# Sample rows' projections on four 32-column tiles, and attention products that alternate the two key/value heads

## The chip, the cores and the metric

The kernel runs on one core of one Trainium2 chip. The metric is the time of one execution in device microseconds (us). Engines: PE (TensorE, matrix products), DVE (VectorE), ACT (ScalarE), POOL (GpSimd, here the issuer of the row gathers) and SP (SyncE, the issuer of the weight loads).

## The reference

One decoder layer for 512 prompt rows and 8 sample rows (one new token for each of eight sequences with a cache), all in float32, width 1024. Cut to what matters:

```python
sh1,sc1,g1,sh2,sc2,g2 = split6(silu(c) @ w_ada + b_ada)      # adaLN, one vector per sequence
h  = rms_norm(x) * (1+sc1) + sh1
q, k, v, p, ga, gb = split(h @ w_in)                         # 512, 128, 128, 512, 1024, 1024 columns
A  = sliding-window attention, 8 query heads on 2 key/value heads, head width 64, window 128
B  = multi-scale causal pooling of p
x  = x + g1 * ((sigmoid(ga)*(A@w_branch_attn) + sigmoid(gb)*(B@w_branch_pool)) @ w_out)
h2 = rms_norm(x) * (1+sc2) + sh2
x  = x + g2 * peer(h2)     # 8 heads x 16 experts a row, each a gathered row of two 16384 x 1024 tables
```

## The kernel before

**Stages.** The prompt is four blocks of 128 rows (`NB = 4`), the sample rows are a fifth block of eight (`rows(NB) = 8`). Activations for products lie transposed: `hT[:, k, cols(b)]` is the k-th of eight 128-row pieces of the width, for the columns of block b. The first part, to about 413 us, does adaLN, the projections, attention, pooling, the branches and the output projection of the first half of the prompt (256 rows), and the expert choice of the first heads. The second part gathers 1040 expert rows by indirect DMA from POOL, in an order fixed by index, while VectorE forms dot products and PE sums the expert rows (line 1531, on four 64 x 64 tiles) and does the second half's products.

**Order.** Every engine's program is written out by hand, and PE is in order. Results of PE go to eight PSUM banks in turn: `bank_plan()` lists all tiles in PE's order with the engine that empties them ("A" ScalarE, "V" VectorE), and `begin(key)` makes PE wait until the content eight places back is emptied. `wait_emptied` and `wait_filled` wait for one tile. Weights come in 2 MB chunks through a ring of three slots (`weight_chunks`, SP's loop, lines 462 to 483): SP, in order, loads a chunk as soon as the chunk three before in its slot has had its last product.

**Projections** (PE lines 1284 to 1292). For each of q, kv and p, five blocks; a block is eight products over k with `hT` as the stationary operand and 512 (kv: 256) weight columns streaming. The sample block streams the same columns for a stationary operand of eight columns. ScalarE copies each block out (line 591, the helper `empty`). Then the gate products (line 1296, by the helper `pass_product`, whose matmuls are on line 1227), two 128-row gates by two between the later steps. A float32 matmul is two instructions in the trace.

**q and k normalisation.** When all kv blocks are out, VectorE squares and sums (lines 902 to 904), ScalarE takes a root after the first four gates (line 632), VectorE multiplies (906 to 911) and sets `qk_normed`, which PE awaits on line 1299 before it transposes q and k, and POOL before its window stores.

**Attention of a block b.** PE makes scores (line 1318: operands of 64 rows, since a head is 64 wide; key/value head 0 lies on partitions 0 to 63, head 1 on 64 to 127). VectorE adds the bias into `sS[b % 2]` (922), finds maxima (928 to 931), ScalarE exponentiates eight heads (643), VectorE normalises (939). PE then transposes the probabilities ("pt", 1340), ScalarE copies them to `pT`, and PE multiplies them with the values ("o", 1344), 64 output partitions a head, and only then turns to the other head, since both use one `pT`. On PE the order is scores(1), pooled(1), gates, values(0), scores(2), and so on.

**Samples.** Scores with the cached keys ("sc4", line 1390), pooled branch ("y", 1401), branch products with the weights `wa` and `wb`, then the value products of the samples ("os", lines 1422 and 1423, 4 columns each, the second for the oldest cached row), adaLN chunk 7 and the output projection.

**The adaLN products** (line 1245) are already packed: `scT` has 32-column pieces, product k goes to output partitions 32 (k % 4) and up, so that four products lie side by side in the array, and `ada` (line 1253) adds the four partial sums by a product with the 0/1 matrix at `K_SEL`.

## Time and profile before

| | |
|---|---|
| median of 3 runs | 1910.24 us (1908.02 to 1910.49) |
| the profiled execution | 1913.8 us |
| its span, first to last instruction | 1911.9 us |
| PE busy | 1327.0 us, 69% |
| DVE busy | 1108.7 us, 58% |
| POOL busy | 1108.0 us, 58% |
| ACT busy | 258.6 us, 14% |
| mean granted TensorE clock | 0.82 of 2.4 GHz |

Busy shares are means over both parts of the kernel, whose limits differ. A line number is that of the program above; line 591 is ScalarE's helper for all copies out of PSUM and line 1227 PE's helper for most products, so their instructions are told apart by their place in time and their shape. The chain of work that ended last is followed back from the last instruction; a piece of PE in it means that PE, not a wait, set the time there.

### The profile page before, as it was taken

The page shows a single profiled execution, that of the slowest core. Times are in us where ns is not written, and L with a number is a line of the kernel's source. Part 1 is how long each engine was busy: PE and PEld are TensorE (multiplying, and loading weights), DVE is VectorE, ACT ScalarE, POOL GpSimd, SP SyncE. Part 2 cuts the span into 40 slices and gives each one's busy share as a digit, 9 for nine tenths or more (in the row PEclk, how much of TensorE's full clock was granted, in tenths as well). Part 3 has the DMA queues.
Part 4 walks back from the last instruction along what each step waited for, and adds up shares of the span by engine and source line. Part 5 has one row for each costly group of instructions (what it writes and reads, how often), then busy time and mean ns, then how long its engine had stood idle before and what let it go on. Part 6 is the DMA issues. An engine that isn't in the chain of part 4 may idle for free.

```text
span 1911.9 us, 19507 instructions
## 1 busy us (share of the span) xinstructions
PE 1327.0 (69%) x7067; PEld 672.8 (35%) x7067; DVE 1108.7 (58%) x2613; ACT 258.6 (14%) x489; POOL 1108.0 (58%) x1066
## 2 busy tenths in 40 slices
PE   5999899896778857645877655556555547764567
PEld 3547667585344423213444211111111112211122
DVE  5013331267656667767557667767777666686540
ACT  2114430221111100111111101000000011100000
POOL 1201000036766677765677777777777777777773
PEclk8999897798799978788889876676667788777769
DMA  9334143869999999997999999999999999999996
GB/s 329 109 100 148 60 137 110 306 244 318 374 372 403 373 399 405 400 404 277 387 371 379 389 408 397 400 377 404 355 407 407 406 405 408 408 370 362 388 409 268
DMA packets 196265, 639.21 MB, mean 334 GB/s; under 512 B 21856, under 2 KB 23188, under 8 KB 196042
## 3 DMA queue, kind: packets, MB, share of 16 engines
q0 software_dynamic: 154992, 550.65, 74.6%
q1 hardware_dynamic: 41178, 87.31, 13.1%
q8 instruction: 57, 0.93, 0.2%
q14 instruction: 38, 0.31, 0.0%
HBM read 634.09 MB, written 3.59 MB: 334 GB/s over the span
## 4 chain that ended last, share of the span: by engine, by line
POOL 36%; PE 30%; DMA 15%; issue 12%; DVE 4%; ACT 2%; SPq 0%; DVEq 0%; POOLq 0%; ACTq 0%
POOL arena L543 36%; PE psum L1227 12%; DMA arena<-in_peer_v,arena 10%; PE psum L1531 7%; PE psum L1291 5%; DMA arena<-in_peer_u,arena 3%; PE psum L1245 1%; ACT arena L591 1%; DVE arena L1121 1%; DMA arena<-in_w_ada 1%; ACT arena L643 1%; PE psum L1318 1%; DMA arena<-in_w_in 1%; PE psum L1557 0%; DMA arena<-in_x_sample 0%
## 5 line engine op out<-in xcount | busy, mean ns | idle before, releaser
L1531 PE MATMUL psum<-arena 64*64 64x512 f32 x4096 | 665.9, 800 | 489.3 <-DMA arena<-in_peer_v,arena 474.6
L1121 DVE CUSTOM_DVE_ANT_0 arena<-arena 128x1024 f32<-128x1024 f32 x520 | 635.1, 1227 | 431.1 <-DMA arena<-in_peer_u,arena 413.4
L543 POOL DMA_INDIRECT arena<-in_peer_v,arena x520 | 548.3, 1054 | 228.2 <-issue 145.0
L543 POOL DMA_INDIRECT arena<-in_peer_u,arena x520 | 533.9, 1027 | 227.7 <-issue 155.4
L1531 PEld LDWEIGHTS psum<-arena 64*64 64x64 f32 x4096 | 202.6, 179 | 931.3 <-issue 914.2
L1227 PE MATMUL psum<-arena 128*128 128x264 f32 (+3 forms) x1620 | 382.7, 394 | 15.3 <-ACT arena L591 15.0
L1227 PEld LDWEIGHTS psum<-arena 128*128 128x128 f32 (+1 forms) x1620 | 304.2, 194 | 92.3 <-issue 41.7
L591 ACT ACTIVATE arena<-psum 128x512 f32<-128x512 f32 (+9 forms) x219 | 91.7, 447 | 492.1 <-PE psum L1227 281.1
L728 ACT ACTIVATE arena<-arena 128x16 f32<-128x16 f32 x32 | 6.9, 217 | 836.6 <-DVE arena L1121 836.6
L1291 PE MATMUL psum<-arena 128*128 128x512 f32 (+3 forms) x240 | 88.5, 528 | 2.9 <-DMA arena<-in_w_in 2.9
L1291 PEld LDWEIGHTS psum<-arena 128*128 128x128 f32 (+1 forms) x240 | 40.7, 172 | 49.9 <-issue 42.9
L538 POOL DMA_DIRECT2D arena<-in_cache_v x1 | 0.5, 537 | 87.6 <-PE psum L1401 87.6
L540 POOL DMA_DIRECT2D arena<-in_consts x1 | 0.6, 589 | 78.3 <-PE psum L1436 78.3
L1121 DVE DVE_READ_ACCUMULATOR2_ANT arena<- 128x1 f32 x520 | 43.0, 83 | 0.0
L1135 DVE TENSOR_TENSOR arena<-arena 128x512 f32<-128x512 f32 x64 | 41.6, 691 | 1.1
L728 ACT ACT_TABLE_LOAD x32 | 41.1, 1283 | 0.2
L726 ACT ACT_TABLE_LOAD x31 | 39.8, 1283 | 0.5
L1046 DVE MAX8 arena<-arena 128x8 f32<-128x128 f32 (+3 forms) x99 | 29.8, 329 | 17.1 <-ACT arena L591 16.9
L523 POOL DMA_DIRECT2D arena<-arena x2 | 1.1, 544 | 61.8 <-DVE arena L911 61.8
L848 DVE TENSOR_TENSOR arena<-psum,arena 128x36 f32<-128x36 f32 x12 | 2.3, 195 | 59.5 <-PE psum L1253 59.5
L922 DVE SCALAR_TENSOR_TENSOR arena<-psum,arena 128x512 f32<-128x512 f32 (+1 forms) x16 | 9.4, 622 | 46.8 <-PE psum L1318 46.7
L1245 PE MATMUL psum<-arena 128*32 128x512 f32 x192 | 29.8, 752 | 8.5 <-DMA arena<-in_w_ada 8.5
(197 smaller groups left out, 852.0 us busy)
## 6 DMA issues: line engine op xcount, KB each, us to landing
arena<-in_w_ada SPq DMA_DIRECT2D x12, 2048.0 KB, 12.3
arena<-in_w_in SPq DMA_DIRECT2D x10, 2048.0 KB, 14.6
arena<-in_peer_wq SPq DMA_DIRECT2D x8, 2048.0 KB, 14.2
arena<-in_peer_u,arena POOLq DMA_INDIRECT x520, 6.6
arena<-in_peer_v,arena POOLq DMA_INDIRECT x520, 7.1
arena<-in_w_out SPq DMA_DIRECT2D x4, 2048.0 KB, 14.2
arena<-in_w_branch_attn SPq DMA_DIRECT2D x4, 1024.0 KB, 11.4
arena<-in_w_branch_pool SPq DMA_DIRECT2D x2, 2048.0 KB, 12.0
```

Of the source, the lines that this page charges most:

```text
L543: pool.indirect_dma_start(out=rows_to, out_offset=None, in_=table[0], in_offset=bass.IndirectOffsetOnAxis(ap=index, axis=0)).then_inc(land ...
L591: ins = act.activation(out, in_, f, **kw)
L643: act.activation(sS[b % 2][:, h, lo:], sS[b % 2][:, h, lo:], ACT.Exp, bias=nmax[:, h:h + 1], accum_out=ssum[:, h:h + 1])
L726: act.activation(v, v, ACT.Exp)
L728: act.activation(acts[:, u % 2, :], acts[:, u % 2, :], ACT.Gelu_apprx_tanh).then_inc(gelu_done, 1)
L1046: dve.max(v[:, 0:8], s)
L1121: dve.tensor_tensor_reduce(rows_r, rows_r, h, 1.0, 0.0, ALU.mult, ALU.add, total).then_inc(u_used, 1)
L1135: dve.tensor_tensor(diags[n % 4], halves_on[:, HW:2 * HW].unsqueeze(1).broadcast_to((P, 8, HW)), coefs[:, 8 * f:8 * f + 8].unsqueeze(2).br ...
L1227: ins = pe.matmul(out, a, b, start=(n == 0), stop=(n == len(pairs) - 1))
L1245: ins = pe.matmul(o[k % 4 * 32:(k % 4 + 1) * 32, :], scT[:, k, :], w[:, k, :], start=(k < 4), stop=(k >= 4), skip_group_check=True)
L1291: ins = pe.matmul(o, hT[:, k, cols(b)], wt[:, k, 0:n], start=(k == 0), stop=(k == C - 1))
L1531: ins = pe.matmul(psum[i * HW:(i + 1) * HW, 2 * g + h, :], diags[n % 4][ps, k + i, :], v_rows[v_buf[r]][ps, h * 512:(h + 1) * 512], start= ...
```

## The change

The sample block of q, kv and p is no longer eight full products. The eight sample rows are copied into `h_padded`, eight pieces of 32 columns whose last 24 are zero; product k goes to output partitions 32 (k % 4) and up ("parts"), ScalarE copies the four partial results into `ada_rows`, and one product with the 0/1 matrix `kc[:, K_SEL:K_SEL + S]` adds them (`sample_sums`). The sum of q comes after kv's parts, that of kv after p's parts, that of p after the first gate product.

Scores of the two key/value heads alternate, each head in its own banks; VectorE takes the four score tiles in the order 0, 2, 1, 3. `values(b)` is split: `turned(b)` transposes the probabilities of both heads, and ScalarE keeps them in two `pT` buffers; `values(b)` then multiplies both heads, alternating, into one bank. Between them stand the scores and the pooling of the next block, or other products. The samples' scores and value products alternate the heads as well. What is computed stays the same. In the diff, the same steps written out in ScalarE's program and in the samples' scores are left out (...).

```diff
@@ -55,6 +55,7 @@
 PLACES = UNITS + 1
 AT_A, AT_B, AT_O2, AT_SK, AT_SS, AT_MEAN, AT_NORM, AT_H2N, AT_PQ = 8, 16, 26, 36, 37, 38, 39, 41, 42
 HW = 64
+KV_TURNS = (0, 2, 1, 3)
 
 
 K_ID = 0
@@ -122,30 +123,38 @@
     plan += [(("xT", c), "A") for c in range(C)] + [(("xTs",), "A")]
     plan += ada_rows(0) + [(("ss", 1, h), "V") for h in both]
     plan += ada_rows(1) + ada(0) + ada_rows(2) + ada(1) + ada_rows(3) + ada(2) + ada(3)
-    plan += [((w, b), "A") for w in ("q", "kv", "p") for b in range(NB + 1)]
-
     def gates(ms):
         return [(("gate", m, 0), "A") for m in ms]
 
+    for w, before in (("q", None), ("kv", "q"), ("p", "kv")):
+        plan += [((w, b), "A") for b in range(NB)] + [(("parts", w), "A")]
+        plan += [((before, NB), "A")] if before else []
+    plan += gates((0,)) + [(("p", NB), "A")]
+
     def scores(b):
-        return [(("s", b, j), "V") for j in range(G)]
+        return [(("s", b, j), "V") for j in KV_TURNS]
+
+    def turned(b):
+        halves = (1,) if b == 0 else (0, 1)
+        return [(("pt", b, kv, h), "A") for kv in range(KV) for h in halves]
 
     def values(b):
-        halves = (1,) if b == 0 else (0, 1)
-        return [k for kv in range(KV) for k in [(("pt", b, kv, h), "A") for h in halves] + [(("o", b, kv), "A")]]
+        return [(("o", b), "A")]
 
     def subkeys(h):
         return [(("skT", h, i), "A") for i in range(4)]
 
-    plan += gates(range(8))
+    plan += gates(range(1, 8))
     for b in range(NB):
         plan += [(("qT", b), "A"), (("kT", b), "A")]
     plan += [(("qkTs",), "A")]
-    plan += scores(0) + [(("d", 0), "A")] + gates((8, 9)) + scores(1) + [(("d", 1), "A")] + gates((10, 11)) + values(0)
-    plan += scores(2) + [(("d", 2), "A")] + gates((12, 13)) + values(1) + scores(3) + [(("d", 3), "A")] + gates((14, 15)) + values(2)
-    plan += [(("ds",), "A")] + ada_rows(4) + values(3) + ada(4) + ada_rows(5) + ada_rows(6) + ada(5) + ada(6)
+    plan += scores(0) + [(("d", 0), "A")] + gates((8, 9)) + scores(1) + [(("d", 1), "A")] + gates((10, 11))
+    plan += turned(0) + scores(2) + [(("d", 2), "A")] + values(0) + gates((12, 13))
+    plan += turned(1) + scores(3) + [(("d", 3), "A")] + values(1) + gates((14, 15))
+    plan += turned(2) + [(("ds",), "A")] + ada_rows(4) + values(2)
+    plan += turned(3) + ada(4) + ada_rows(5) + values(3) + ada_rows(6) + ada(5) + ada(6)
     plan += [(("ktT", i), "A") for i in range(2)] + [(("k0T",), "A")]
-    plan += [(("sc4", kv, h), "V") for kv in range(KV) for h in range(2)] + [(("sc0", kv), "V") for kv in range(KV)]
+    plan += [(("sc4", kv, h), "V") for h in range(2) for kv in range(KV)] + [(("sc0", kv), "V") for kv in range(KV)]
     plan += [(("y", g, h), "A") for h in both for g in range(PG)]
     plan += [((w, n, 0), "V") for n in range(C) for w in ("A", "B")]
     plan += [(("pts",), "A"), (("os",), "A")] + ada_rows(7) + ada(7)
...
@@ -315,7 +324,8 @@
     o_q = take(5184)
     zsq, qk_rms = at(o_q, 3200), at(o_q + 3200, 50)
     sS = [at(o_q, 2048, 8), at(o_q + 2048, 2048, 8)]
-    pT = at(o_q + 4096, 1024, 2)
+    pT = [at(o_q + 4096, 1024, 2), at(o_gt, 1024, 2)]
+    h_padded = at(o_q + 4096, C * 32, C)
     ktile = at(o_keep + G * late[1], 1024, S)
     vtile = at(take(1024), 1024, S)
     kTs = at(o_q + 2048, 1024, S)
@@ -614,20 +624,38 @@
         for i in range(1, 4):
             ada(i)
         act.wait_ge(filler_ready, 1)
-        for b in range(NB + 1):
+        def queries(b):
             out = zqk[0:rows(b), b, 0:512].rearrange("p (j v e) -> p v j e", v=KV, e=HD)
             copy(("q", b), out, bank(("q", b))[0:rows(b)].rearrange("p (v j e) -> p v j e", v=KV, e=HD))
-        for b in range(NB + 1):
+
+        def keys_values(b):
             src = bank(("kv", b))[0:rows(b)]
             empty(("kv", b), [(zqk[0:rows(b), b, 512:640], src[:, 0:128], ACT.Copy, {}),
                               (zv[0:rows(b), b, :], src[:, 128:256], ACT.Copy, {})])
-        for b in range(NB + 1):
+
+        def pool_inputs(b):
             copy(("p", b), zp[0:rows(b), b, :], bank(("p", b))[0:rows(b)])
+
         def gates(ms):
             for m in ms:
                 copy(("gate", m, 0), (ga0 if m < C else gb0)[:, m % C, :], bank_half(("gate", m, 0), 0), ACT.Sigmoid)
 
-        gates(range(4))
+        for b in range(NB):
+            queries(b)
+        wait_filled(act, ("ada", 3))
+        copy(("parts", "q"), ada_rows[0], bank(("parts", "q")))
+        for b in range(NB):
+            keys_values(b)
+        copy(("parts", "kv"), ada_rows[1][:, 0:256], bank(("parts", "kv"))[:, 0:256])
+        queries(NB)
+        for b in range(NB):
+            pool_inputs(b)
+        wait_filled(act, ("q", NB))
+        copy(("parts", "p"), ada_rows[0], bank(("parts", "p")))
+        keys_values(NB)
+        gates((0,))
+        pool_inputs(NB)
+        gates(range(1, 4))
         act.wait_ge(qk_mean_ready, 1)
         act.activation(qk_rms, qk_rms, ACT.Sqrt).then_inc(qk_root_ready, 1)
         gates(range(4, 8))
@@ -644,15 +672,15 @@
                                accum_out=ssum[:, h:h + 1])
             act.activation(ssink, ssink, ACT.Exp).then_inc(exps_ready, 1)
 
+        def turned(b):
+            if b:
+                wait_filled(act, ("o", b - 1))
+            for kv in range(KV):
+                for h in ((1,) if b == 0 else (0, 1)):
+                    copy(("pt", b, kv, h), pT[kv][:, h, :], bank(("pt", b, kv, h)))
+
         def values(b):
-            halves = (1,) if b == 0 else (0, 1)
-            for kv in range(KV):
-                if b or kv:
-                    wait_filled(act, ("o", b, 0) if kv else ("o", b - 1, 1))
-                for h in halves:
-                    copy(("pt", b, kv, h), pT[:, h, :], bank(("pt", b, kv, h)))
-                r = slice(kv * HD, (kv + 1) * HD)
-                copy(("o", b, kv), (att0, att1)[b // 2][r, :, cols(b % 2)], bank(("o", b, kv))[r].rearrange("p (a b) -> p a b", a=G))
+            copy(("o", b), (att0, att1)[b // 2][:, :, cols(b % 2)], bank(("o", b)).rearrange("p (a b) -> p a b", a=G))
 
         def pooled(b):
             copy(("d", b), dT[:, :, cols(b)], bank(("d", b)).rearrange("p (a b) -> p a b", a=PG))
...
@@ -863,7 +895,7 @@
         def modulate_samples(shift):
             hs = hT[:, :, T:TT]
             link(dve.tensor_tensor(hs, hs, smod[:, :, 1:9], ALU.mult))
-            dve.tensor_tensor(hs, hs, mods[:, shift:shift + C, 1:9], ALU.add)
+            return dve.tensor_tensor(hs, hs, mods[:, shift:shift + C, 1:9], ALU.add)
 
         def modulate(shift, cs):
             for c in range(C):
@@ -889,7 +921,9 @@
             ada(i)
         wait_emptied(dve, ("ada", 3))
         scales(C, 48)
-        modulate_samples(0)
+        dve.memset(h_padded, 0.0)
+        link(modulate_samples(0))
+        dve.tensor_copy(h_padded[:, :, 0:S], hT[:, :, T:TT])
         modulate(0, slice(0, T))
         wait_emptied(dve, ("xTs",))
         dve.memset(zqk[:, NB, :], 1.0).then_inc(filler_ready, 1)
@@ -917,14 +951,14 @@
             lo = P if b == 0 else 0
             if b >= 2:
                 wait_filled(dve, ("pt", b - 2, 1, 1))
-            for j in range(G):
+            for j in KV_TURNS:
                 wait_filled(dve, ("s", b, j))
                 dve.scalar_tensor_tensor(sS[b % 2][:, 2 * j:2 * j + 2, lo:], bank(("s", b, j)).rearrange("p (v s) -> p v s", v=KV)[:, :, lo:],
                                          HD ** -0.5, bias[:, 2 * j:2 * j + 2, lo:], ALU.mult, ALU.add).then_inc(emptied_by_dve, 1)
 
         def maxima(b):
             lo = P if b == 0 else 0
-            wait_emptied(dve, ("s", b, G - 1))
+            wait_emptied(dve, ("s", b, KV_TURNS[-1]))
             link(dve.tensor_reduce(nmax, sS[b % 2][:, :, lo:], X, ALU.max))
             link(dve.tensor_tensor(nmax, nmax, sinks, ALU.max))
             link(dve.tensor_scalar(nmax, nmax, -1.0, None, ALU.mult))
...
@@ -1281,21 +1315,36 @@
             ada_products(i)
             ada(i - 1)
         ada(3)
+        def sample_sums(w, parts):
+            o = begin((w, NB))
+            wait_emptied(pe, ("parts", w))
+            end(pe.matmul(o[0:S, 0:parts.shape[1]], kc[:, K_SEL:K_SEL + S], parts, start=True, stop=True))
+
         for w, n in (("q", 512), ("kv", 256), ("p", 512)):
             wt = chunk((w,))
-            for b in range(NB + 1):
-                o = begin((w, b))[0:rows(b), 0:n]
+            for b in range(NB):
+                o = begin((w, b))[:, 0:n]
                 for k in range(C):
                     if (w, b) == ("q", 0):
                         pe.wait_ge(h_ready, k + 1)
                     ins = pe.matmul(o, hT[:, k, cols(b)], wt[:, k, 0:n], start=(k == 0), stop=(k == C - 1))
                 end(ins)
+            o = begin(("parts", w))[:, 0:n]
+            for k in range(C):
+                ins = pe.matmul(o[k % 4 * 32:(k % 4 + 1) * 32, :], h_padded[:, k, :], wt[:, k, 0:n], start=(k < 4), stop=(k >= 4), skip_group_check=True)
+            end(ins)
+            if w == "kv":
+                sample_sums("q", ada_rows[0])
+            if w == "p":
+                sample_sums("kv", ada_rows[1][:, 0:256])
 
         def gates(ms):
             for m in ms:
                 pass_product(("gate", m, 0), 0, chunk(("gate", m // 4, 0)), m % 4, hT[:, :, half(0)], C)
 
-        gates(range(8))
+        gates((0,))
+        sample_sums("p", ada_rows[0])
+        gates(range(1, 8))
         pe.wait_ge(qk_normed, 1)
         for b in range(NB):
             o = begin(("qT", b))
@@ -1311,13 +1360,15 @@
         def scores(b):
             wait_emptied(pe, ("kT", b))
             lo = P if b == 0 else 0
-            for j in range(G):
-                o = begin(("s", b, j))
-                r = slice(j // 2 * HD, (j // 2 + 1) * HD)
+            for j in range(2):
+                o = [begin(("s", b, kv * 2 + j)) for kv in range(KV)]
                 for i in range(2):
-                    ins = pe.matmul(o[:, i * 2 * P + lo:(i + 1) * 2 * P], qkT[r, j % 2 * 2 + i, cols(b)],
-                                    qkT[r, 4, (b - 1) * P + lo:(b + 1) * P], start=True, stop=True)
-                end(ins)
+                    for kv in range(KV):
+                        r = slice(kv * HD, (kv + 1) * HD)
+                        ins = pe.matmul(o[kv][:, i * 2 * P + lo:(i + 1) * 2 * P], qkT[r, j * 2 + i, cols(b)],
+                                        qkT[r, 4, (b - 1) * P + lo:(b + 1) * P], start=True, stop=True)
+                        if i == 1:
+                            end(ins)
 
         def pooled(b):
             own = K_OWN if b else K_FIRST
@@ -1330,18 +1381,24 @@
                 ins = product(o[:, gs], pairs)
             end(ins)
 
-        def values(b):
-            halves = (1,) if b == 0 else (0, 1)
+        def turned(b):
             pe.wait_ge(probs_ready, b + 1)
             for kv in range(KV):
-                for h in halves:
+                for h in ((1,) if b == 0 else (0, 1)):
                     o = begin(("pt", b, kv, h))
                     for j in range(G):
                         ins = pe.transpose(o[:, j * P:(j + 1) * P], sS[b % 2][:, kv * G + j, h * P:(h + 1) * P], ident)
                     end(ins)
-                o = begin(("o", b, kv))
-                wait_emptied(pe, ("pt", b, kv, 1))
-                end(product(o[kv * HD:(kv + 1) * HD, :], [(zv[:, b - 1 + h, kv * HD:(kv + 1) * HD], pT[:, h, :]) for h in halves]))
+
+        def values(b):
+            halves = (1,) if b == 0 else (0, 1)
+            o = begin(("o", b))
+            wait_emptied(pe, ("pt", b, 1, 1))
+            for h in halves:
+                for kv in range(KV):
+                    r = slice(kv * HD, (kv + 1) * HD)
+                    ins = pe.matmul(o[r, :], zv[:, b - 1 + h, r], pT[kv][:, h, :], start=(h == halves[0]), stop=(h == 1), skip_group_check=True)
+            end(ins)
 
         pe.wait_ge(consts_loaded, 16)
         scores(0)
@@ -1350,15 +1407,17 @@
         scores(1)
         pooled(1)
         gates((10, 11))
-        values(0)
+        turned(0)
         scores(2)
         pooled(2)
+        values(0)
         gates((12, 13))
-        values(1)
+        turned(1)
         scores(3)
         pooled(3)
+        values(1)
         gates((14, 15))
-        values(2)
+        turned(2)
         pe.wait_ge(tail_loaded, 32)
         o = begin(("ds",))
         for g in range(PG):
@@ -1366,9 +1425,11 @@
                             start=True, stop=True)
         end(ins)
         ada_products(4)
-        values(3)
+        values(2)
+        turned(3)
         ada(4)
         ada_products(5)
+        values(3)
         ada_products(6)
         ada(5)
         ada(6)
...
@@ -1414,13 +1476,16 @@
         pe.wait_ge(oldest_v_loaded, 16)
         o = begin(("os",))
         wait_emptied(pe, ("pts",))
-        for kv in range(KV):
-            r = slice(kv * HD, (kv + 1) * HD)
-            for s in range(S):
-                i = (kv * S + s) * G
-                out = o[r, s * G:(s + 1) * G]
-                pe.matmul(out, vtile[:, s, r], pTs[:, i:i + G], start=True, stop=False)
-                ins = pe.matmul(out, v0[0:1, s, r], pTs[0:1, 64 + i:64 + i + G], start=False, stop=True)
+        for s in range(S):
+            for oldest in range(2):
+                for kv in range(KV):
+                    r = slice(kv * HD, (kv + 1) * HD)
+                    i = (kv * S + s) * G
+                    out = o[r, s * G:(s + 1) * G]
+                    if oldest:
+                        ins = pe.matmul(out, v0[0:1, s, r], pTs[0:1, 64 + i:64 + i + G], start=False, stop=True, skip_group_check=True)
+                    else:
+                        ins = pe.matmul(out, vtile[:, s, r], pTs[:, i:i + G], start=True, stop=False, skip_group_check=True)
         end(ins)
         ada_products(7)
         ada(7)
```

## Rows read from the trace of the kernel before

**Rows 1.** Page, part 4: shares of the span in the chain, by engine

```profile
POOL 36%; PE 30%; DMA 15%; issue 12%; DVE 4%; ACT 2%; SPq 0%; DVEq 0%; POOLq 0%; ACTq 0%
```

**Rows 2.** The chain in order of time: start us, length us, what

```profile
132.40 27.82 PE psum L1227 x128
...
205.52 4.04 ACT arena L643 x16
...
271.97 27.95 PE psum L1227 x128
...
351.93 16.69 DMA arena<-in_w_ada
```

**Rows 3.** PE, attention: start, length, line, operation, shapes, count [idle before <- releaser]

```profile
172.38 2.96 PE L1318 MATMUL psum<-arena 64*128 64x256 f32 x16
...
187.95 1.94 PE L1227 MATMUL psum<-arena 128*64 128x512 f32 x2 [3.28 <-ACT arena L591]
...
193.65 5.65 PE L1318 MATMUL psum<-arena 64*128 64x256 f32 x16
...
237.83 3.43 PE L1227 MATMUL psum<-arena 128*64 128x512 f32 x4 [4.54 <-ACT arena L591]
```

**Rows 4.** Stages: length; busy us of PE, PEld, DVE, ACT, POOL; clock; DMA share; GB/s

```profile
162.80:262.10 99.30, 85.10 (x414) 58.68 (x414) 28.93 (x46) 45.84 (x117) 3.57 (x5) 0.88 0.35 104
187.40:204.00 16.60, 15.21 (x43) 10.06 (x44) 6.57 (x8) 3.48 (x5) 0.00 (x0) 0.50 0.39 137
303.00:323.00 20.00, 19.13 (x92) 14.49 (x92) 0.20 (x1) 0.80 (x2) 0.00 (x0) 0.50 0.68 237
480.00:1020.00 540.00, 382.38 (x2173) 200.95 (x2166) 353.90 (x863) 65.37 (x117) 369.72 (x353) 0.85 0.98 379
```

**Rows 5.** Groups, 30 to 420 us: value products; busy, mean ns | idle before, releaser

```profile
L1227 PE MATMUL psum<-arena 128*64 128x512 f32 x28 | 17.8, 764 | 14.2 <-ACT arena L591 14.2
```

**Rows 6.** ScalarE in order of time: copies of q's block 3 and its sample block

```profile
73.20 0.61 ACT L591 ACTIVATE arena<-psum 128x512 f32<-128x512 f32 x1 [6.27 <-PE psum L1291]
80.17 0.59 ACT L591 ACTIVATE arena<-psum 8x512 f32<-8x512 f32 x1 [6.37 <-PE psum L1291]
```

**Rows 7.** PE in order of time: adaLN products and the three input projections

```profile
34.29 1.92 PE L1245 MATMUL psum<-arena 128*32 128x512 f32 x16
36.15 1.06 PE L1253 MATMUL psum<-arena 128*128 128x9 f32 x8
37.13 1.93 PE L1245 MATMUL psum<-arena 128*32 128x512 f32 x16
...
43.91 88.49 PE L1291 MATMUL psum<-arena 128*128 128x512 f32 x240 [2.95 <-DMA arena<-in_w_in]
```

**Rows 8.** VectorE in order of time: modulation, and the end of q/k normalisation

```profile
41.90 3.74 DVE L870 TENSOR_SCALAR arena<-arena 128x512 f32<-128x512 f32 x8
...
156.28 0.29 DVE L911 TENSOR_TENSOR arena<-arena 128x128 f32<-128x128 f32 x1
```

**Rows 9.** The chain in order of time: one expert sum of 16 instructions

```profile
506.77 1.92 PE psum L1531 x16
```

**Rows 10.** SP in order of time: the load of the pooled branch's weights

```profile
258.57 0.38 SPq L483 DMA_DIRECT2D arena<-in_w_branch_pool  x1
```

**Rows 11.** DMA issues to 420 us: count, KB each, median us to landing

```profile
arena<-in_w_branch_pool SPq DMA_DIRECT2D x1, 2048.0 KB, 9.3
```

**Rows 12.** PE in order of time: the samples' scores

```profile
263.86 2.92 PE L1390 MATMUL psum<-arena 64*4 64x128 f32 x29 [0.66 <-ACT arena L591]
```

**Rows 13.** The chain: first two pairs and last pair of the samples' value products

```profile
301.91 0.25 PE psum L1422 x2
302.16 0.20 PE psum L1423 x2
...
310.87 0.30 PE psum L1423 x2
```

35 lines of the change are left out of this document (20 added, 15 removed).

## The prediction

> **What bounds the kernel now.** I read the chain that ended last first, as shares and then in order of time. POOL's row gathers and the DMAs behind them hold about half of the span, but they own the second part of it, from about 413 us. The change touches nothing there. Up to 413 us the chain runs almost wholly on PE, in long pieces with no wait inside: 88.49 us for the three input projections, then 27.82 us for eight gate products [rows 1, 2, 7]. So time taken from PE before 413 us reaches the end, unless a DMA or another engine is late instead; the chain has one long DMA piece there, 16.69 us for an adaLN weight chunk, and that load is issued when PE frees its slot, so it moves with PE [rows 2]. Then I read PE's order of time and the stretch 162.8 to 262.1 us, the attention. There PE is busy for 85.10 of 99.30 us at a mean granted clock of 0.88 [rows 3, 4]. The reader is to see two losses besides the work: waits, above all PE waiting for ScalarE's copies of the turned probabilities (3.28 us once, 4.54 us once, 14.2 us over all value products [rows 5]), and stretches at 1.2 GHz that begin just after such waits.
>
> **Sample rows' projections.** Before, the eight sample rows cost eight matmuls (16 instructions, as float32 makes two passes) of full width. ScalarE's copies show it: from the copy of q's block 3 to that of the sample block it is 80.17 - 73.20 = 6.97 us [rows 6]; p is as q, and kv with 256 columns half, 3.49 us. Removed: 6.97 + 3.49 + 6.97 = 17.4 us. Added: 16 instructions on four 32-column tiles, which the adaLN products already do in 1.92 us for 512 columns [rows 7]; q and p cost that, kv half, 0.96, together 4.8 us. Then one 128-row matmul for each to add the four partial sums: two instructions of 6.97/16 = 0.436 us, 0.87 us for q and p, 0.43 for kv, together 2.2 us. Switching between four tiles and the full array shows no gap (1.92, 1.06, 1.93 us back to back [rows 7]), so it is nothing, at most 0.1 us for each of six switches. Net: 17.4 - 4.8 - 2.2 = **10.4 us**, all on the path.
>
> What is added elsewhere. VectorE gets a clearing, a step wait and a small copy before the rows that PE needs first, some 0.6 us. PE starts at 43.91 us after a DMA wait of 2.95 us, and the eight modulating instructions began at 41.90, 0.47 us each [rows 7, 8]; 0.6 us later they still keep ahead of PE's pace of 0.436 us or slower. Without that cover it would cost 0.6 us. ScalarE copies three more tiles, under PE's products. The kv sample rows now arrive after p instead of before it, and the normalisation of q and k hangs on them. Its last multiply ended at 156.57 us, before PE wanted it at 160.2 [rows 2, 8]. But the root was queued on ScalarE behind the fourth gate then and is so now, and the squares (some 7 us, of three gate products of 3.48 us) are done by then; gates and chain move together, so the 3.6 us of slack stays. POOL's first window stores wait for the same event and move with it.
>
> **Attention.** Four effects, at the two heads' 64-row and 64-column tiles.
> First, work that is halved. Scores of a block are 16 instructions of 256 columns, 27.82/128 = 0.217 us each [rows 2]; the trace has 2.96 us at full clock, since the two heads overlap once [rows 3]. Alternating, I take 8 x 0.217 + 0.1 = 1.84 us, a gain of 1.1 us for each of three blocks and 0.55 for the first: 3.9 us. Value products of a block are 8 instructions of 512 columns, 3.49 us, and become 1.74: 1.75 x 3 + 0.87 = 6.1 us. That two 64-wide tiles really overlap, I take from the expert sums, 64 x 64 tiles of 512 columns: 16 instructions in 1.92 us instead of 16 x 0.436 = 7.0 [rows 9]. Bounds: nothing, or all **10.0 us**.
> Second, waits. Of the 14.2 us before value products [rows 5], almost all goes: the turning of block b is followed by the scores of block b + 1, not by a product that needs ScalarE's copies. What is late next is PSUM: eight banks go round, and the scores of block 3 need the banks of the pooled tile and the gates that ScalarE empties only after its exponentials of block 2. Before, block 2's scores began at 193.65 and its exponentials ended at 209.56 [rows 2, 3], 16 us, some 13 with the scores at full clock, and three more copies follow. PE's work between the two blocks' scores is about as long (gates 7, pooling, values and turning 5). So it waits there for 1 to 3 us, and again for the copies before value product 2. I leave 3.3 us of waits and take 14.2 - 3.3 = **10.9 us**; bounds 0 (all waits come back as bank waits) and 14.2.
> Third, the clock. At 0.88 mean, 0.12 x 99.3 = 11.9 us of full speed were not granted; in the long stretch 187.4 to 204 at 0.50 PE worked for 15.21 of 16.60 us [rows 4], so about 0.92 x 11.9 = 10.9 us is lost work. It fell after the 3.28 us wait and after the 4.54 us wait. With no wait over about 1.5 us left, I expect 2.4 GHz, save one short stretch of some 3.3 us (1.6 us lost): **9.3 us**; bounds 0 and 10.9.
> Fourth, moved steps. Each scores call takes its banks in pairs, and VectorE takes heads in the order 0, 2, 1, 3: no more work. ScalarE's copies of values go out as one of 128 partitions, not two of 64, four fewer. SP's queue: gate and adaLN chunks are released by the same products, in the same order, earlier. The nearest is the pool-branch weights, issued at 258.57 when an adaLN product ended, landing 9.3 us later, at 267.9, while the first branch product ran at 271.97 [rows 2, 10, 11], 4.1 us of slack. The adaLN product that frees it keeps its distance from the branch products, so I count nothing; 0 to 3 us if it is late.
> Sum of the section: 10.0 + 10.9 + 9.3 = 30.2 us.
>
> **Sample attention.** The scores of the samples take 2.92 us [rows 12] and become about 1.5: **1.4 us**, since ScalarE's copies of the pooled branch follow them. The value products of the samples are 64 instructions of 4 columns from 301.91 to 311.17, 9.26 us, a pair for 0.30 us at 1.2 GHz, for 0.25 and 0.20 at the start, still at 2.4 [rows 13]. The cost is hardly the columns. Alternating can overlap the two heads' fixed costs or leave them: 0 to 4.6 us. The nearest rows with alternating tiles are the adaLN products, which overlap, but with 512 columns; I take the middle, **2.3 us**. [...]
>
> **Sum.** 10.4 + 30.2 + 1.4 + 2.3 = 44.3 us. The profiled execution took 1913.8 us (its span 1911.9): 1869.5 after. The median of the runs shown is 1910.24, 3.6 us less, so the forecast is **1866 us**, if the gather part simply starts 44 us earlier. It keeps its own pace: its DMA share is 0.98 in 480 to 1020 us [rows 4].
>
> **Rivals.**
> A, the clock stays as low in the attention as before, because the transposes and small copies starve PE all the same: 9.3 us less gain, 35.0, so 1875 us. For it: 303 to 323 us is at 0.50 with PE busy 19.13 of 20 us [rows 4], so a busy PE alone does not keep it up. Against: every fall in the attention followed a wait.
> B, the change does not do what it says: alternating 64-wide tiles do not overlap. 10.0 + 1.4 + 2.3 less, 30.6 us of gain, 1880 us. Against it speak the expert sums [rows 9].
> C, the four-column value products of the samples gain nothing, as their fixed cost is issued one after the other: 2.3 less, 1868 us. The pair cost of 0.30 us for 4 columns speaks for it. [...]
> D, the clock does not fall at 303 us: shorter sample values end before it. Of 19.13 us of busy time some 8 go, 1858 us. Little speaks for it.
> E, the waits come back as bank waits on ScalarE: 10.9 less, 1877 us. The bank rotation speaks for it; that PE's work between two blocks' scores is as long as ScalarE's chain, against.
> F, slower than before: in 480 to 1020 us PE's late products and expert sums fall to the low clock. PE is busy there for 382.38 of 540 us at 0.85 [rows 4], 325 us of work at full clock; at 0.50 that is 650 us, 110 more than the stretch. It eats the 44 us once the mean falls below 325/584 = 0.56. Nothing in the change leads there; it would need a shifted start to settle in a worse pattern.
>
> **How the numbers follow.** Chances: forecast 0.38, A 0.18, B 0.06, C 0.20, D 0.08, E 0.08, F 0.02. The range 1856 to 1881 takes in all but F and the outer ends of A, B and E when they add up, with about 3 us for terms that are off and the runs' spread of 2.5 us. A change of 0.2%, 3.8 us, is about what a measurement of this kernel can tell from none. Only F, or several rivals at once, come near it: faster 0.96, same 0.02, slower 0.02.
>
> **What would show it.** Right: the sample part of each projection at about 1.9 us (kv 1.0) with sums of 0.9 or less, and the first gate product group ending about 10 us earlier; scores of a full block near 1.8 us and values near 1.9; idle before value products under 4 us in all; mean granted clock over the attention near 0.98; branch products starting some 42 us earlier. Wrong: a clock near 0.88 there (A), scores still near 3 us (B), new PE waits on ScalarE before scores (E), sample values still 9 us (C), or a gather part that is longer than before, which my sum holds unchanged.

## The result, and the profile after

| | before | after |
|---|---|---|
| median, first comparison (4 runs each) | 1909.33 us (1908.02 to 1910.49) | 1861.14 us (1854.46 to 1867.89) |
| ratio, with its 95% interval | | 0.9745 (0.9705 to 0.9786) |
| ratio, second comparison (13 and 4 runs) | | 0.9775 (0.9714 to 0.9836) |
| the profiled execution, its span | 1913.8, 1911.9 us | 1855.26, 1853.3 us |

The change makes the kernel 48 us faster (2.5%); 44.3 us, to 1866 us, was forecast, with a range of 1856 to 1881. The interval of the second comparison reaches to 0.9836, so it does not show by itself that the gain is over 2%. The spans of the two profiled executions lie 58.6 us apart, more than the medians. So the difference is followed by marks in the trace, stage by stage, and later over all traces.

The span and the chain's shares by engine, from the page of after, answer to [rows 1]:

```profile
span 1853.3 us, 19523 instructions
...
POOL 41%; PE 27%; issue 14%; DMA 13%; DVE 3%; ACT 1%; SPq 0%; DVEq 0%; POOLq 0%; ACTq 0%
```

PE's share of the chain is 27% where it was 30%, POOL's 41% where it was 36%. Second traces of both kernels, described below, have 29% and 30% for PE, 37% and 38% for POOL, so these shares tell little of the change. PE of after in order of time, the projections (start, length, line, operation, shapes, count, idle before and its releaser), answers to [rows 7] and, for the sample block, to [rows 6]:

```profile
46.86 29.71 PE L1330 MATMUL psum<-arena 128*128 128x512 f32 x64 [7.20 <-DMA arena<-in_w_in]
76.50 1.93 PE L1334 MATMUL psum<-arena 128*32 128x512 f32 x16
78.36 14.08 PE L1330 MATMUL psum<-arena 128*128 128x256 f32 x64
92.37 1.07 PE L1334 MATMUL psum<-arena 128*32 128x256 f32 x16
93.26 1.02 PE L1321 MATMUL psum<-arena 128*8 128x512 f32 x2
...
121.93 1.93 PE L1334 MATMUL psum<-arena 128*32 128x512 f32 x16
123.67 0.59 PE L1321 MATMUL psum<-arena 128*8 128x256 f32 x2
...
153.08 0.60 PE L1352 MATMUL psum<-arena 128*128 128x128 f32 x4
...
155.76 1.16 PE L1368 MATMUL psum<-arena 64*128 64x128 f32 x16
```

The sample block of q takes 1.93 us for the parts and, a stage later, 0.95 for the sum (from 93.26 to the next product at 94.21), where it was 6.97. No gap shows where the tiling changes. From the first projection to the first score it is 155.76 - 46.86 = 108.90 us; before, 162.74 - 43.91 = 118.83. **9.9 us**, of 10.4 forecast.

The end of the q and k normalisation on VectorE, for the cover that the prediction counted on [rows 8]:

```profile
149.29 0.29 DVE L945 TENSOR_TENSOR arena<-arena 128x128 f32<-128x128 f32 x1
```

It ends at 149.58, PE wants it at 153.08: 3.5 us of slack, as forecast (3.6).

PE of after, the attention, answers to [rows 3 and 5]:

```profile
164.85 2.00 PE L1368 MATMUL psum<-arena 64*128 64x256 f32 x16
...
176.54 2.28 PE L1368 MATMUL psum<-arena 64*128 64x256 f32 x16
179.29 2.05 PE L1261 MATMUL psum<-arena 128*128 128x128 f32 x16 [0.47 <-ACT arena L601]
181.27 1.08 PE L1400 MATMUL psum<-arena 128*64 128x512 f32 x4
...
191.13 1.14 PE L1368 MATMUL psum<-arena 64*128 64x256 f32 x8
192.97 1.13 PE L1368 MATMUL psum<-arena 64*128 64x256 f32 x8 [0.70 <-ACT arena L601]
194.03 2.05 PE L1261 MATMUL psum<-arena 128*128 128x128 f32 x16
196.01 1.94 PE L1400 MATMUL psum<-arena 128*64 128x512 f32 x8
...
210.06 1.94 PE L1400 MATMUL psum<-arena 128*64 128x512 f32 x8 [0.61 <-ACT arena L601]
...
223.90 1.93 PE L1451 MATMUL psum<-arena 64*4 64x128 f32 x32 [0.66 <-ACT arena L601]
...
231.00 27.95 PE L1261 MATMUL psum<-arena 128*128 128x256 f32 x128 [0.78 <-ACT arena L601]
```

Scores of a block take 2.00 us instead of 2.96 (2.28 in block 2), the value products of both heads 1.94 us. The 14.2 us of waits before value products are gone; what is new are three waits for ScalarE, 0.47 + 0.70 + 0.61 = 1.8 us. The prediction had named two of them, in the scores of block 3 (0.70) and before the value products of block 2 (0.61). The stage by windows (length, busy us of PE, PEld, DVE, ACT, POOL, clock, DMA share, GB/s) answers to [rows 4]:

```profile
155.80:222.00 66.20, 64.41 (x413) 48.51 (x413) 28.53 (x46) 42.22 (x114) 3.56 (x5) 1.00 0.50 147
434.00:974.00 540.00, 381.04 (x2172) 202.26 (x2176) 349.23 (x855) 64.45 (x117) 370.00 (x351) 0.85 0.98 376
```

The granted clock is 1.00 of 2.4 GHz where it was 0.88. From the first scores to the branch products it is 231.00 - 155.76 = 75.24 us instead of 271.97 - 162.74 = 109.23: **34.0 us**, with the sample scores in it, of 31.6 forecast. In the middle of the gather part clock, PE time and DMA share are as before.

The samples' value products in the chain of after (start, length, what; four instructions are now two matmuls, one of each head), as [rows 13]:

```profile
260.93 0.28 PE psum L1488 x4
261.21 0.21 PE psum L1486 x4
...
264.97 0.31 PE psum L1486 x4
265.28 3.62 PE psum L1279 x16
```

Four instructions take what two took: 4.35 us instead of 9.26, **4.9 us** of 2.3 forecast. Last, the first expert gather on POOL, in before and then in after:

```profile
400.82 1.02 POOL L543 DMA_INDIRECT arena<-in_peer_u,arena  x1 [49.92 <-DVE arena L1094]
```

```profile
347.27 1.03 POOL L553 DMA_INDIRECT arena<-in_peer_u,arena  x1 [46.05 <-DVE arena L1128]
```

Gathers begin 53.6 us earlier. Of that, stages which the change touches give 9.9 + 34.0 + 4.9 = 48.8, less 3.0 for weights that came later in this execution (46.86, not 43.91). Some 7.7 us came in stages behind them which the change leaves alone, and 5.0 more after the first gather (1911.9 - 400.82 = 1511.1 us against 1506.0). The table at the end of the experiments shows that these last two vary from trace to trace. In what follows "after" or "changed" is this kernel.

### The profile page after: what moved, and what is told of

It is laid out like the page before. It is cut to its first block, busy times and chain, and to the rows that moved or that the text cites. A ratio compares the mean times of both kernels' runs of the same rounds, so it can differ in the third digit from the quotient of the medians.

```text
span 1853.3 us, 19523 instructions
## 1 busy us (share of the span) xinstructions
PE 1286.3 (69%) x7073; PEld 650.6 (35%) x7073; DVE 1107.4 (60%) x2615; ACT 255.0 (14%) x488; POOL 1103.7 (60%) x1066
## 3 DMA queue, kind: packets, MB, share of 16 engines
q0 software_dynamic: 154992, 550.65, 76.9%
q1 hardware_dynamic: 41178, 87.31, 13.5%
## 4 chain that ended last, share of the span: by engine, by line
POOL 41%; PE 27%; issue 14%; DMA 13%; DVE 3%; ACT 1%; SPq 0%; DVEq 0%; POOLq 0%; ACTq 0%
POOL arena L553 41%; PE psum L1261 12%; DMA arena<-in_peer_v,arena 9%; PE psum L1596 6%; PE psum L1330 4%; DMA arena<-in_peer_u,arena 2%; PE psum L1279 1%; DMA arena<-in_w_in 1%; DVE arena L1155 1%; ACT arena L601 1%; DMA arena<-in_w_ada 1%; DMA arena<-in_x_sample 0%; PE psum L1622 0%; PE psum L1287 0%; PE psum L1508 0%
## 5 line engine op out<-in xcount | busy, mean ns | idle before, releaser
L1596 PE MATMUL psum<-arena 64*64 64x512 f32 x4096 | 673.9, 809 | 481.4 <-DMA arena<-in_peer_v,arena 467.1
L1596 PEld LDWEIGHTS psum<-arena 64*64 64x64 f32 x4096 | 206.4, 180 | 927.4 <-issue 911.0
L1261 PE MATMUL psum<-arena 128*128 128x264 f32 (+2 forms) x1592 | 358.4, 383 | 1.8 <-ACT arena L601 1.8
L1261 PEld LDWEIGHTS psum<-arena 128*128 128x128 f32 x1592 | 295.4, 191 | 71.5 <-issue 25.4
L601 ACT ACTIVATE arena<-psum 128x512 f32<-128x512 f32 (+6 forms) x218 | 88.6, 447 | 458.1 <-PE psum L1261 271.1
L1330 PE MATMUL psum<-arena 128*128 128x512 f32 (+1 forms) x192 | 71.6, 533 | 7.2 <-DMA arena<-in_w_in 7.2
L1330 PEld LDWEIGHTS psum<-arena 128*128 128x128 f32 x192 | 36.9, 193 | 41.7 <-issue 32.7
L758 ACT ACT_TABLE_LOAD x31 | 39.8, 1283 | 0.5
L1080 DVE MAX8 arena<-arena 128x8 f32<-128x128 f32 (+3 forms) x99 | 29.8, 328 | 14.6 <-ACT arena L601 14.3
L1183 DVE TENSOR_TENSOR arena<-psum,arena 128x512 f32<-128x512 f32 x16 | 9.9, 679 | 39.9 <-PE psum L1596 39.9
```

The lines of the kernel that those rows point to most:

```text
L601: ins = act.activation(out, in_, f, **kw)
L758: act.activation(v, v, ACT.Exp)
L1080: dve.max(v[:, 0:8], s)
L1183: dve.tensor_tensor(scaled[i], psum[:, i, :].rearrange("p (a b) -> p a b", a=2), g2b[:, h].rearrange("p (a b) -> p a b", a=2), ALU.mult).t ...
L1261: ins = pe.matmul(out, a, b, start=(n == 0), stop=(n == len(pairs) - 1))
L1330: ins = pe.matmul(o, hT[:, k, cols(b)], wt[:, k, 0:n], start=(k == 0), stop=(k == C - 1))
```

## The experiments

**The changed kernel again**, to see its spread.

> The changed kernel once more. Its four times so far lie in two pairs, 1855 and 1867 us, while those of before stay within 2.5 us. If the start of the program makes the difference (the first projection waited for its weights until 46.86 us instead of 43.91), a longer execution has its gathers begin later than 359.6 us by as much. If the gather part makes it, the gathers begin at 359.6 us within 4 us in every execution and the rest differs by up to 13 us. Expected here: 1861 us, ratio 0.970 to 0.979.

1860.35 us in the median, 1853.23 to 1868.22; in these runs the kernel before went from 1894.93 to 1920.33. (The gather start of 359.6 us in this expectation and the next is the seventh gather of after; the text counts from the first, at 347.27.) The trace agrees with the first one in every stage of the first part within 0.3 us, and the first gather comes 300.8 us after the first projection, as in the first trace (300.4). Both traces are of short executions, so what a long one does differently was not seen, and the question of the expectation stays open. By the two intervals above, total times resolve 8 to 12 us here; the marks of the first three stages resolve 1 to 3.

**Each part alone.**

```diff
 # attention_only: projections as before
-    for w, before in (("q", None), ("kv", "q"), ("p", "kv")):
-        plan += [((w, b), "A") for b in range(NB)] + [(("parts", w), "A")]
+    plan += [((w, b), "A") for w in ("q", "kv", "p") for b in range(NB + 1)]
 # projections_only: the same hunks applied to the kernel before, nothing else
```

> The projections as before (sample block as eight full products), all of the attention as changed. My sum: the projections' 10.4 us come back (9.9 by the trace), and nothing else, so 1871 us and a gather start of about 369.5. Rival, the projections' gain is lost later (a weight load or ScalarE sets the time): 1861 us, as the changed kernel.

> The sample rows on four 32-column tiles, the attention as before. My sum: 10.4 us faster than before, 1899 us, with PE's waits before value products at 14 us and a mean clock of about 0.88 over the attention, as before. Rival, the earlier start alone makes the attention's clock better: 1890 us or less.

attention_only: 1867.28 us, ratio to before 0.979 (0.9734 to 0.9846), of 1871 expected; from the first projection to the first gather 310.4 us, 10.0 more than the changed kernel. projections_only: 1893.49 us, ratio 0.994 (0.9909 to 0.997); to the first score 109.5 us, as changed, and then 107.5 us of attention at a clock of 0.92, 1.7 and 2.9 us less than in the two traces of before (0.89 and 0.88). So the rival, a better clock by the earlier start alone, has at most these 2 to 3 us. By the marks the two parts add up: 9.3 us of projections and 33.5 us of attention, each against the first trace of before, 42.9 together, against 43.9 for the whole change. The projections' 10 us reach the gathers undiminished. The medians can't show this: they give 40.5 + 14.3 = 54.8 us against 47.5. The expectation of 1899 us for projections_only missed by 5.5, and its trace does not explain that, since the execution that was traced took 1904.53 us.

**Heads in turn**, to size the overlap of the two heads apart from the order of steps.

```diff
-KV_TURNS = (0, 2, 1, 3)
+KV_TURNS = (0, 1, 2, 3)      # scores head by head, as before
-            for h in halves:
-                for kv in range(KV):
+            for kv in range(KV):          # values head by head
+                for h in halves:
 # the samples' scores and value products head by head as well
```

> The changed kernel with its new order of steps and two buffers, but the two heads one after the other in scores, value products and both sample products, so that two 64-wide tiles seldom stand side by side. My sum: 10.0 + 1.4 + 2.3 us come back, and with the sample values as long as before the clock stays low into the output projection, some 5 us more, so 1875 to 1880 us, with full-block scores near 3 us and value products near 3.7. Rival, the filled waits and the clock alone bring the gain of the attention: 1861 to 1865 us.

1866.17 us, ratio 0.9787 (0.9731 to 0.9842). PE, the scores of a block, its value products, and the samples' scores:

```profile
165.86 2.96 PE L1367 MATMUL psum<-arena 64*128 64x256 f32 x16
...
198.68 1.95 PE L1398 MATMUL psum<-arena 128*64 128x512 f32 x8
...
226.03 3.50 PE L1449 MATMUL psum<-arena 64*4 64x128 f32 x29 [0.66 <-ACT arena L601]
```

Scores are back at 2.96, but the value products still take 1.95 us for eight instructions of 0.43: the heads overlap although they don't alternate. From first scores to branch products it is 78.5 us, 3.3 more than changed, 1.6 of them in the samples' scores. Of these 1.6, 0.6 are the clock's and not the overlap's: the same instructions took 2.92 us at 2.4 GHz in before [rows 12] and 3.50 here, where the granted clock is 0.50 from 226 to 229 us. Of 3.4 us saved on the prompt's scores (11.1 us of instructions here, 7.7 in the changed kernel) only some 1.7 reach the branch products: this kernel has none of the three waits of 1.8 us that the changed one has. That is the prediction's rival E, in small. The samples' value products cost 4.4 us. 1866 lies under the 1875 to 1880 expected, as the clock fell no longer into the output projection than in the changed kernel (27.98 us in both); the traced execution took 1873.53 us, with the first gather 10.8 us later than in the changed kernel.

**Values at once**, to give the waits back.

```diff
-        turned(0)
-        scores(2)
-        pooled(2)
-        values(0)
+        turned(0)
+        values(0)
+        scores(2)
+        pooled(2)
 # blocks 1 to 3, ScalarE and the bank plan in the same way
```

> The changed kernel with each block's value products right behind its transposes, as before, and the next block's scores after them; tiles still alternate, both heads still in one step. My sum: the waits for ScalarE's copies come back (before they were 3.3, 2.1 and 4.5 us for the first head of a block, and 0.9 elsewhere, some 11 us in all), and with them stretches at 1.2 GHz (up to 9 us lost). From the first scores to the branch products 75.2 us becomes 86 to 95, the mean clock there falls to about 0.9, the first gather starts at 358 to 368 us, the time is 1870 to 1880 us. Rival, the overlap of the two heads is the gain and the order of steps matters little: within 4 us of the changed kernel at each of these places.

1878.9 us, ratio 0.985 (0.9805 to 0.9894); the first gather is 21.2 us later than changed. PE before the value products, and the stage:

```profile
181.05 1.89 PE L1400 MATMUL psum<-arena 128*64 128x512 f32 x4 [4.03 <-ACT arena L601]
...
201.62 3.63 PE L1400 MATMUL psum<-arena 128*64 128x512 f32 x8 [5.28 <-ACT arena L601]
...
223.10 3.68 PE L1400 MATMUL psum<-arena 128*64 128x512 f32 x8 [5.28 <-ACT arena L601]
```

```profile
156.00:252.40 96.40, 79.38 (x505) 57.45 (x505) 34.52 (x57) 47.81 (x127) 4.04 (x6) 0.91 0.44 134
```

The stage takes 96.2 us instead of 75.2, 1.2 more than the expectation allowed. The waits before value products are back, 15.6 us with the last of 1.0, and behind each of the long ones the same product runs at 1.2 GHz (3.63 instead of 1.94). The tiles alternate all the same, so this is the price of the order of steps: 21.0 us, the largest part of the gain.

**The waits filled, in the kernel before**, to take the clock apart from the waits.

```diff
                 o = begin(("o", b, kv))
+                for _ in range((4, 3, 6, 1)[b] if kv == 0 else 1):
+                    pe.matmul(o[kv * HD:(kv + 1) * HD, :], ident[:, 0:HD], kc[:, K_BIAS:K_BIAS + 512], start=True, stop=True)
                 wait_emptied(pe, ("pt", b, kv, 1))
```

> The kernel before, with matmuls of constants put into PE's waits before the value products, written to the bank that the product then overwrites; they are sized to end about when ScalarE's copies do. If the waits make the clock fall, it stays at 2.4 GHz over the attention (mean 0.97 or more instead of 0.89), and from the first scores to the branch products it takes some 100 us instead of 109.2: the clock's share of the gain alone. Rival, the clock falls for another reason: mean near 0.89 and 109 us or more.

1899.08 us, ratio 0.9963 (0.9933 to 0.9994). The stage from the first scores to the branch products, in this kernel and in the second trace of before:

```profile
165.00:267.00 102.00, 98.84 (x541) 64.67 (x541) 35.86 (x57) 51.04 (x130) 4.10 (x6) 1.00 0.44 137
```

```profile
164.50:274.80 110.30, 93.96 (x502) 65.34 (x502) 35.74 (x57) 50.78 (x129) 4.02 (x6) 0.88 0.41 126
```

Work without use in the waits keeps the clock at 1.00, and the stage shrinks from 109.2 and 110.4 to 101.7 us: the clock is worth 7.5 to 8.7 us there, with the order of steps and the useful work as they were. It may be worth a little more, since in block 2 the added matmuls ended some 0.7 us after the copy that PE waits for. The falls of the clock in the attention came from the waits.

**The samples' value products in turn.**

```diff
-        for s in range(S):
-            for oldest in range(2):
-                for kv in range(KV):
+        for kv in range(KV):
+            for s in range(S):          # then the cached rows and the oldest row, as before
```

> The changed kernel with the samples' value products head after head, as before. By the trace they went from 9.26 to 4.35 us, so this kernel has 4.9 us more there, and starts gathers at 352.5 us if nothing after them changes. By my sum it would be 2.3 us, by the fixed cost being issued one after the other nothing.

One execution, 1859.28 us, too few to tell 5 us by. From the branch products to the output projection it is 43.9 us instead of 39.6, and the first gather is 305.5 us after the first projection instead of 300.4: 4.3 and 5.1 us. The term is confirmed at about twice the forecast.

**The kernel before again**, for a second trace.

> The kernel before once more, for a second trace. In five traces of changed kernels the projections began at 46.9 to 47.3 us, in that of before at 43.91. If that was chance, this trace has about 47 as well, with the first gather 3 us later than 400.82; if the change delays the first weights, it has 43.9 again.

The projections began at 44.16 us, close to the first trace's 43.91, which by the expectation would speak for a delay by the change. The other traces speak against it. attention_only and before_filled have the start of the kernel before and began at 47.15 and 46.37 us, while four kernels with the changed projections began at 44.5, 44.7, 44.9 and 45.5. So the 3 us are chance of the weights' arrival. The added work on VectorE shows once, in longer_sum below, where weights came early and the idle time before the first projection ended on VectorE. The first gather came at 397.60, 3.2 us earlier than in the first trace, although the attention took 1.1 us longer: the stage from the output projection to the first gather took 77.6 instead of 83.5 us.

**Sums at once**, to see what the delayed sums hide.

```diff
-            if w == "kv":
-                sample_sums("q", ada_rows[0])
-            if w == "p":
-                sample_sums("kv", ada_rows[1][:, 0:256])
+            sample_sums(w, ada_rows[1][:, 0:256] if w == "kv" else ada_rows[0])
 # the sum of p, the bank plan and ScalarE in the same way
```

> The changed kernel with each projection's partial sums added right behind its own parts, not one stage later. PE then waits for ScalarE's copy of the parts (0.6 us and the hand-overs, 0.2) three times: 2.4 us. From the start of the projections to the first scores 109.0 us becomes 111.4. Rival: PE's queue holds nothing to hide and the clock falls in these waits, 114 or more.

```profile
77.96 1.02 PE L1319 MATMUL psum<-arena 128*8 128x512 f32 x2 [0.87 <-ACT arena L600]
...
94.59 0.59 PE L1319 MATMUL psum<-arena 128*8 128x256 f32 x2 [0.60 <-ACT arena L600]
...
125.62 1.02 PE L1319 MATMUL psum<-arena 128*8 128x512 f32 x2 [0.87 <-ACT arena L600]
```

0.87 + 0.60 + 0.87 = 2.3 us, as expected; to the first score it is 112.5 us, 3.5 more than changed, 1.0 of it in q's products, which began at the low clock. The one execution took 1867.9 us. It is no measure of 2.3 us: the first gather is 12 us later than in the changed kernel, and 6.2 of these lie between the output projection and the gathers, 1.4 in the samples' scores, which ran at 1.2 GHz.

**A longer sum**, to see whether PE's time reaches the gathers.

```diff
-            end(pe.matmul(o[0:S, 0:parts.shape[1]], kc[:, K_SEL:K_SEL + S], parts, start=True, stop=True))
+            for _ in range(13 if w == "p" else 1):
+                ins = pe.matmul(o[0:S, 0:parts.shape[1]], kc[:, K_SEL:K_SEL + S], parts, start=True, stop=True)
+            end(ins)
```

> The changed kernel with the matmul that adds p's partial sums done thirteen times instead of once, 12 x 0.87 = 10.4 us more of PE and nothing else. If PE's time ahead of the gathers reaches them undiminished, from the start of the projections to the first gather 300.6 us becomes 311.0. Rival, a weight load or the gathers' own preparation takes part of it: under 308. The gather part keeps its 1503 to 1516 us in either case.

```profile
126.21 11.32 PE L1322 MATMUL psum<-arena 128*8 128x512 f32 x26
```

The first score is 119.7 us after the first projection, 10.8 more; the attention then takes 75.3 us, as in the changed kernel. At the first gather it is 314.6, 14.0 more. The added time is passed on whole, and 2.6 us come from the output projection, which ran 30.56 instead of 27.98 us. One execution, 1865.15 us.

**Sub-keys earlier**, an attempt at a version faster than both.

```diff
-    chunks += [(("wo", 0, 0), ("o2", 3, 0)), (("wo", 1, 0), ("o2", 7, 0)), (("sk", 0), ("skT", 0, 3))]
+    chunks += [(("wo", 0, 0), ("o2", 3, 0)), (("sk", 0), ("skT", 0, 3)), (("wo", 1, 0), ("o2", 7, 0))]
         for n in range(C):
+            if n == 4:
+                subkeys(0)
             pass_product(("o2", n, 0), 0, chunk(("wo", n // 4, 0)), n % 4, mT0, C)
 # the later subkeys(0) goes; the bank plan and ScalarE in the same way
```

> The changed kernel with the sub-key transposes in the middle of the output projection and their weights loaded before the second half of w_out, so that two adaLN chunks load earlier. In the changed kernel PE and VectorE lie on the chain from 298.6 to 325.1 us for these chunks, 9.3 us of it a DMA wait. If that load sets the time, the first gather comes 5 to 9 us earlier, counted from the start of the projections (292 to 296 instead of 300.6), and the time is 1851 to 1856 us. Rival, the four chunks are bound by the DMA's rate wherever they start: 300 and 1860.

1855.18 us (1848.81 to 1859.44), ratio to before 0.9712 (0.968 to 0.9743), an interval that overlaps that of the changed kernel. The first gather is 300.7 us after the first projection, as in the changed kernel. PE's waits for the adaLN weights, in this kernel and in after:

```profile
311.31 3.64 PE L1280 MATMUL psum<-arena 128*32 128x512 f32 x16 [2.77 <-DMA arena<-in_w_ada]
316.71 3.42 PE L1280 MATMUL psum<-arena 128*32 128x512 f32 x16 [1.76 <-DMA arena<-in_w_ada]
```

```profile
307.98 3.64 PE L1279 MATMUL psum<-arena 128*32 128x512 f32 x16 [5.79 <-DMA arena<-in_w_ada]
```

The wait moved from the second chunk to the third and fourth. Counted from the first projection, SP issued the four loads at 237.9, 251.8, 253.5 and 255.4 us in after, and at 241.5, 243.2, 257.1 and 259.0 here. So only the second load went out earlier, and landed 6.0 us sooner; the third and fourth went out 3.6 us later and landed 0.7 us sooner, and PE waits for those. The edit thus did not bring the four loads forward, and whether their issue or the DMA's rate sets the time is not shown. The part of the output projection before the transposes also ran partly at the low clock here (16.61 us for half of it), so a gain of 2 to 3 us may be covered; a better version is not shown.

**Runs of four**, since the heads in turn had overlapped in one place and not in others.

```diff
-                for i in range(2):
-                    for kv in range(KV):
+                for kv in range(KV):
+                    for i in range(2):      # scores; values and the samples' values in the same way
```

> The changed kernel with the heads alternating in runs of two matmuls (four instructions) instead of one (two instructions), in scores, prompt values and sample values. In the kernel with the heads in turn the value products, whose runs are four instructions long, still took 1.95 us for both heads, as when alternating, while full-block scores (runs of eight) took 2.96 instead of 2.00 and sample values (runs of 32) 4.3 us more. If PE looks some instructions ahead for one that its other tile can take, runs of four cost nothing: scores 2.0, values 1.9, sample values 4.4. If alternation itself is needed, scores are 2.6 or more and sample values 6 or more.

```profile
164.12 2.10 PE L1368 MATMUL psum<-arena 64*128 64x256 f32 x16
...
195.41 1.95 PE L1400 MATMUL psum<-arena 128*64 128x512 f32 x8
...
223.30 3.40 PE L1451 MATMUL psum<-arena 64*4 64x128 f32 x32 [0.65 <-ACT arena L601]
...
261.80 0.25 PE L1488 MATMUL psum<-arena 128*64 128x4 f32 x2 [0.50 <-ACT arena L601]
261.98 0.27 PE L1486 MATMUL psum<-arena 1*64 1x4 f32 x2
...
270.20 3.64 PE L1279 MATMUL psum<-arena 128*32 128x512 f32 x16
```

Neither theory holds throughout. Scores (2.10 us) and values lose next to nothing in runs of four. The samples' values take 8.4 us, from 261.80 to 270.20: no overlap. What differs is the neighbour: in the changed kernel a product over 128 rows is followed by one over 128 rows of the other head, here by one over a single row. The Trainium skill, TensorEngine Tiling (Array Packing), section Key Properties, says that changing the tiling mode, and not only the tile, drains the engine. This trace would fit it, as far as 128-row and 1-row products are different modes, though no gap shows where 32-column tiles and the full array follow each other (1.92, 1.06, 1.93 us back to back [rows 7]); a run that tells this from another cause was not made. The samples' scores, which this edit leaves as in the changed kernel, took 3.40 us instead of 1.93, at 1.2 GHz. One execution, 1868.44 us.

**All traces, stage by stage**, in us: from the first projection to the first score (1), to the branch products (2), to the output projection (3), to the first gather (4), to the end (5).

| kernel | 1 | 2 | 3 | 4 | 5 |
|---|---|---|---|---|---|
| before, two traces | 118.8, 120.3 | 109.2, 110.4 | 45.3, 45.1 | 83.5, 77.6 | 1511, 1509 |
| after, two traces | 108.9, 109.2 | 75.2, 75.3 | 39.6, 39.5 | 76.7, 76.8 | 1506, 1503 |
| attention_only | 119.5 | 75.7 | 39.8 | 75.5 | 1516 |
| projections_only | 109.5 | 107.5 | 45.5 | 79.3 | 1514 |
| heads_in_turn | 109.3 | 78.5 | 44.0 | 79.4 | 1513 |
| values_at_once | 109.2 | 96.2 | 39.7 | 76.5 | 1509 |
| before_filled | 118.7 | 101.7 | 44.0 | 75.5 | 1504 |
| sample_values_in_turn | 109.7 | 75.3 | 43.9 | 76.6 | 1507 |
| sums_at_once | 112.5 | 76.7 | 40.2 | 82.8 | 1509 |
| longer_sum | 119.7 | 75.3 | 40.2 | 79.3 | 1504 |
| subkeys_earlier | 109.3 | 75.3 | 40.3 | 75.9 | 1506 |
| runs_of_four | 108.4 | 76.9 | 44.6 | 82.8 | 1507 |

Columns 1 to 3 follow the code within about 1.5 us, but for the 107.5 of projections_only, whose clock in the attention was 0.92. Among the kernels with the changed attention the step of 1.5 us in column 2 is the clock at the samples' scores: seven traces with the alternating scores ran them in 1.93 us, sums_at_once and runs_of_four in 3.29 and 3.40 at a granted clock of 0.5, behind the same wait of 0.65 us. Column 4 is the same code in all but one and runs from 75.5 to 83.5; the output projection alone takes 28.0 us in some traces and 29.6 to 31.0 in others, as a stretch at 1.2 GHz reaches into it or not. Column 5 runs over 13 us without order.

## Why the prediction was right

The mechanism was right: PE held the first part, what left it reached the gathers, and the gather part kept its pace within its chance of 13 us. The size was right within 4 us of 48, less than the totals resolve; by the marks of the first traces the stages that the change touches gained 48.8 us. By its own steps:

- **Projections**: 10.4 forecast, 9.9 in the first pair of traces, 11.1 in the second, 10.0 at the first gather between attention_only and the changed kernel. The covers held: 3.5 us of slack at the normalisation, 2.3 us of copies hidden by the delayed sums. That the work added on VectorE is hidden was right but for one trace.
- **Attention**: 31.6 us forecast with the sample scores, 34.0 measured. By values_at_once the order of steps is worth 21.0 us, where the sum had 10.9 + 9.3 = 20.2 for waits and clock together, and the rest 13.0 (109.2 to 96.2), where it had 10.0 + 1.4 for the overlap. The split of the 20.2 was less good: the clock alone, with the waits filled by work, is 7.5 to 8.7, where it had 9.3, which leaves some 12 to 13.5 for the waits, where it had 10.9. That these two errors, of opposite sign, nearly cancel in the sum is luck. What the prediction had wrong is the part of alternation, to which it put the whole overlap. Alternation is worth 3.3 us, 0.6 of it the clock at the samples' scores, since the value products overlap once both heads stand in one step, alternating or not, and since half of what the scores save comes back as 1.8 us of waits on ScalarE. The terms are not independent: filling a wait saves the wait and the clock behind it, and shortening work in a chain that ScalarE ends opens a new wait.
- **Moved steps**: nothing was counted for the load of the pooled branch's weights, as it would keep its distance from the branch products. It did not quite: landing took 13.2 us instead of 9.3, and 1.2 us of the 4.1 us of slack were left in after. In attention_only the load was late by 0.4 us.
- **Remaining waits and clock**: 3.3 us and one short stretch at 1.2 GHz (1.6 us lost) were left in the sum; 1.8 us of waits and no such stretch were found in both traces of after, with a clock of 1.00. In sums_at_once and runs_of_four there was one, at the samples' scores, and it cost 1.4 and 1.5 us. It came behind a wait of 0.65 us, so that having no wait over 1.5 us is not enough. The length of a wait decides less than the prediction supposed: in before the clock fell also after the wait of 2.08 us (0.52 from 214.0 to 217.3 us), and in projections_only it did not fall after one of 3.08 us. Rival A fell.
- **Samples**: the scores went from 2.92 to 1.93 us of instructions, 1.0 us of 1.4 forecast. The value products are the mis-sized term: 2.3 us, the middle of 0 to 4.6, against 4.3 to 4.9. Fixed costs overlap between the two tiles. Rival C fell with it: here two tiles halve the time of four-column products, though their cost is not their columns.
- **Clock at the samples** (rival D): it fell there again, as the last pairs' 0.31 us show. How far the fall reaches into the output projection (27.98 us in after, 30.96 and 29.55 in before) does not follow the length of the value products: sample_values_in_turn, with long ones, has 27.98 us, sums_at_once, with short ones, 30.57.
- **Slower** (rival F): the clock in the middle of the gather part is 0.85 before and after.

What the sum had no term for is the chance of columns 4 and 5: about 8 us and 13 us between traces of code that is the same there. It made the first pair of traces differ by 58.6 us, where the medians differ by 48. That it is also most of the spread of 13 us in the total is likely, but no long execution of the changed kernel was traced. What decides which level an execution takes in column 4, beyond the clock in the output projection, and what moves the gather part, stays open.
